# Delta rule of a hybrid decoder step: the sample group's state products moved to the first two turns, its new states accumulated in two parts

## The reference

```python
def step(S, inp):
    r_t, w_t, k_t, v_t, kk_t, b_t = inp
    sa = jnp.einsum('bhvk,bhk->bhv', S, kk_t)
    S = S * w_t[:, :, None, :] - sa[..., None] * b_t[:, :, None, :] + v_t[..., None] * k_t[:, :, None, :]
    return S, jnp.einsum('bhvk,bhk->bhv', S, r_t)
```

## Time and profile before

| what | value |
|---|---|
| median of 3 runs | 1483.42 us (1481.92 to 1490.57) |
| profiled execution | 1485.49 us |
| its span, first to last instruction | 1483.7 us |
| mean granted TensorE clock | 0.986 |
| TensorE busy (matmuls) | 1415.4 us, 95% |
| VectorE, ScalarE, GpSimd busy | 798.1, 578.4, 242.3 us |
| delta rule, first matmul to the next stage's first | 490.71 to 879.19 us |

### The profile page before, as it was taken

The page is one execution under the profiler, slowest core; times in us unless marked ns, Lnnn a source line. Parts: engine busy times, 40 slices in busy tenths (PEclk is TensorE's granted clock), DMA queues, the critical chain, the costliest instruction groups (busy, mean ns, idle before and its releaser), DMA issues. The chain is left out here.

```text
span 1483.7 us, 37543 instructions
## 1 busy us (share of the span) xinstructions
PE 1415.4 (95%) x16154; PEld 1284.7 (87%) x16154; DVE 798.1 (54%) x1592; ACT 578.4 (39%) x1182; POOL 242.3 (16%) x343
## 2 busy tenths in 40 slices
PE   7999999999999799999999989999999999998997
PEld 6989898887899799999999848899999997665885
DVE  6737245777821377777777564561111222775545
ACT  6626246887821122221222332441111132886324
POOL 0000000000000355654566230000001000214000
PEclk9999999999999999999999899999999998999999
DMA  5724122567692245434553146024334236431202
GB/s 205 223 59 103 59 89 89 161 174 225 193 261 87 59 110 117 107 86 108 117 117 89 53 149 229 29 78 145 91 98 116 67 119 168 150 103 33 87 29 93
DMA packets 244294, 173.47 MB, mean 117 GB/s; under 512 B 148735, under 2 KB 218303, under 8 KB 243215
## 3 DMA queue, kind: packets, MB, share of 16 engines
q1 hardware_dynamic: 212167, 156.12, 36.6%
q10 hardware_dynamic: 31968, 15.04, 3.5%
HBM read 110.97 MB, written 60.46 MB: 116 GB/s over the span
## 5 line engine op out<-in xcount | busy, mean ns | idle before, releaser
L366 PE MATMUL mix_acc<-mix_high,mix_w_high 128*128 128x364 f32 (+1 forms) x768 | 177.3, 339 | 11.5 <-ACT mix_high L432 10.3
L366 PE MATMUL mix_acc<-mix_low,mix_w_high 128*128 128x364 f32 (+1 forms) x768 | 171.5, 332 | 1.2 <-DVE mix_low L586 1.2
L366 PE MATMUL mix_acc<-mix_high,mix_w_low 128*128 128x364 f32 (+1 forms) x768 | 170.4, 330 | 0.0
L366 PEld LDWEIGHTS mix_acc<-mix_high,mix_w_high 128*128 128x128 f32 x768 | 129.6, 188 | 30.4 <-issue 28.6
L366 PEld LDWEIGHTS mix_acc<-mix_low,mix_w_high 128*128 128x128 f32 x768 | 132.5, 189 | 2.3 <-DVE mix_low L586 2.1
L366 PEld LDWEIGHTS mix_acc<-mix_high,mix_w_low 128*128 128x128 f32 x768 | 133.1, 188 | 0.2 <-DVE mix_w_low L600 0.2
L1482 PE MATMUL out_acc<-qkvg_room_r_high,qkvg_room_w_high 128*128 128x364 f32 (+1 forms) x320 | 105.8, 331 | 2.1 <-DVE qkvg_room_w_low L1834 2.1
L600 DVE TENSOR_TENSOR mix_w_low<-mix_wt,mix_w_high 128x1024 fp32r<-128x1024 f32 x32 | 39.2, 1224 | 124.9 <-ACT mix_w_high L438 124.6
L1482 PE MATMUL out_acc<-qkvg_room_r_low,qkvg_room_w_high 128*128 128x364 f32 (+1 forms) x320 | 105.1, 329 | 0.0
L1482 PE MATMUL out_acc<-qkvg_room_r_high,qkvg_room_w_low 128*128 128x364 f32 (+1 forms) x320 | 105.1, 329 | 0.0
L1832 DVE CAST qkvg_room_w_high<-qkvg_room_wt 128x1024 fp32r<-128x1024 f32 x20 | 14.0, 700 | 155.4 <-DMA qkvg_room_wt<-in_w_att 155.4
(11 more groups left out here) (278 smaller groups left out, 3418.3 us busy)
## 6 DMA issues: line engine op xcount, KB each, us to landing
mix_wt<-in_w_in SPq DMA_DIRECT2D x32, 512.0 KB, 4.6
qkvg_room_wt<-in_w_att SPq DMA_DIRECT2D x20, 512.0 KB, 3.7
delta_bk<-scr_bk SPq DMA_DIRECT2D x17, 512.0 KB, 4.7
delta_kr<-scr_kr SPq DMA_DIRECT2D x17, 512.0 KB, 7.1
scr_kr<-mix_outs SPq DMA_DIRECT2D x16, 512.0 KB, 3.8
scr_bk<-mix_outs SPq DMA_DIRECT2D x16, 512.0 KB, 4.5
early_xpad<-in_xpad SPq DMA_DIRECT2D x8, 548.5 KB, 8.8
scr_xg<-early_xs SPq DMA_DIRECT2D x8, 544.0 KB, 3.0
```

The costliest lines, as they stand in the source:

```text
L366: mm = pe.matmul(acc[:, s, k, 0:width], w[:, s, d, :], r[:, d, n0:n0 + width], start=d == 0 and q == 0, stop=d == DT - 1 and q == 2)
```

## The change

1. The eight loads of `s_sample` leave turns 1 to 8. SyncE issues them in the projections' last jobs, two each at n = 27 to 30 (`follow_slowly`). A copy of chunk 16's kr (`kr_own`, 512 KB) is loaded behind the first operands, at n = 26. `rows`, `s_sample` and `kr_own` move to the memory laid out by `first_of_delta`; `kr_own` shares its place with half of the inverse's buffer.
2. `turn_states` is cut into three: pairs 0 and 1 at the end of turn -1, pairs 2 to 4 and 5 to 7 in turn 0. They write into two banks that are free then, and ScalarE copies each out in turn 0 (`keep_own`). z of chunk 0 waits for the second copy, since it uses the bank.
3. `make_own_states` is cut into the products of v (`own_values`, which open the accumulation) and of u (`own_updates`, which close it). Pairs 0 to 3 of the first stand before and behind z of chunk 16 and behind its u; then come the turning of y 15, y 16, and the products of u.
4. `v_own` is made by GpSimd, in turn 15. All of `u_own` is made by ScalarE.
5. GpSimd scales `s_sample` by one pair at the end of each of turns 1 to 8, instead of all in turn 16.
6. VectorE adds the new states of pairs 0 and 1 before the norm of y 16, 2 and 3 inside it, and the rest behind it with the halves of the next weights. y 15 is turned and gated after z and u of chunk 16, not before.

```diff
+                    if G_ * DT + 2 < n < G_ * DT + 7:
+                        for pair in range(2):
+                            follow_slowly(sp, 2 * (n - (G_ * DT + 3)) + pair)
...
+        sp.dma_start(d["kr_own"][:], scr["kr"][TILES, :, :, :, 0:NB * NT]).then_inc(d["kr_own_loaded"], 16)
+
+    def load_states(sp, pair):
+        sp.dma_start(d["s_sample"][:, pair], a["s_sample"][:, pair]).then_inc(d["s_loaded"], 16)
...
-                    if 1 <= i <= DT:
-                        sp.dma_start(s_sample[:, i - 1], a["s_sample"][:, i - 1]).then_inc(s_loaded, 16)
...
+                    if front == SAMPLE:
+                        pool.wait_ge(v_loaded[SAMPLE % 3], 16 * (SAMPLE // 3 + 1))
+                        for b in range(NB):
+                            own = seq_mask[:, b:b + 1].rearrange("p (j n) -> p j n", j=1).broadcast_to([128, DT, 64])
+                            pool.tensor_tensor(v_own[:, b], v_rows[:, SAMPLE % 3], own, ALU.mult).then_inc(v_owned, 1)
+                    if 1 <= i <= DT:
+                        pair = i - 1
+                        pool.wait_ge(own_made, 2)
+                        end = keep["ends_sample"][:, pair, :].rearrange("p (b o) -> p b o", o=1).broadcast_to([128, NB, 64])
+                        pool.tensor_tensor(s_sample[:, pair], s_sample[:, pair], end, ALU.mult).then_inc(own_ended, 1)
...
                 def make_z(c):
                     if c == 0:
                         pe.wait_ge(zeroed, 3)
-                    elif c < SAMPLE:
-                        pe.wait_ge(s_kept, c)
+                        pe.wait_ge(own_kept, 2)
                     else:
                         pe.wait_ge(s_kept, c)
-                        pe.wait_ge(own_kept, 2)
...
+                def own_values(pairs):
+
+                    if pairs[0] == 0:
+                        pe.wait_ge(solved_wide, SAMPLE + 1)
+                        pe.wait_ge(rows_kept, 2 * SAMPLE + 2)
+                        pe.wait_ge(v_owned, NB)
+                    for pair in pairs:
                         if pair >= 4:
                             pe.wait_ge(own_done, pair - 3)
...
+                        for p in HALVES:
+                            pe.matmul((lm_bank + grown_bank)[pair % 4][p, :], rows[p, SAMPLE % 2, 1, pair, :], v_own[p, :, pair, :], start=True, stop=False)
+
+                def own_updates(pairs):
+                    if pairs[0] == 0:
+                        pe.wait_ge(u_owned, NB)
+                    for pair in pairs:
+                        for p in HALVES:
+                            mm = pe.matmul((lm_bank + grown_bank)[pair % 4][p, :], rows[p, SAMPLE % 2, 0, pair, :], u_own[p, :, pair, :], start=False, stop=True)
                         mm.then_inc(own_s, 1)
...
                     if behind == SAMPLE:
-                        for b in range(NB // 2):
+                        for b in range(NB):
                             act.wait_ge(u_kept, SAMPLE + 1)
                             act.activation(u_own[:, b], u[:], ACT.Copy, scale=seq_mask[:, b:b + 1]).then_inc(u_owned, 1)
...
+                        add_own((0, 1))
                         sum_squares(behind)
                         invert_root(behind)
+                        add_own((2, 3))
                         scale_y(behind)
...
+                        for pair in range(4, DT):
+                            add_own((pair,))
+                            if pair == DT - 1:
                                 gate_y(SAMPLE)
+                            for d in range(2 * pair - DT, 2 * pair - DT + 2):
+                                ahead["rest_of_weights"](dve, d)
```

More of the change, by code:

```diff
@@ L87, with mixed_projections @@
 HALF_K = N // 4
-def mixed_projections(nc, group, a, scr, keep, outp, g_stored, follow):
+def mixed_projections(nc, group, a, scr, keep, outp, g_stored, follow, follow_slowly):
     with Tensors(nc, "mix", group) as m:
@@ L772, in first_of_delta @@
         d["room"] = 8 * DT * 64 + 4 * DT * 64 + 3 * DT * 64 + sum(math.prod(shape) for shape in shapes.values()) + 64
+        d["rows"], d["s_sample"] = m.sb("rows", 128, 2, 2, DT, 64), m.sb("s_sample", 128, DT, NB, 64)
+        d["room"] += 4 * DT * 64 + DT * NB * 64
+        m.sb("inverse", 128, 2 * DT * 64)
+        d["kr_own"] = m.sb("kr_own", 128, 2, DT, 64)
+        d["s_loaded"], d["kr_own_loaded"] = m.sem("s_loaded"), m.sem("kr_own_loaded")
         d["consts_loaded"] = m.sem("consts_loaded")
@@ L799, in delta_rule @@
         kr, bk, v_rows = first["kr"], first["bk"], first["v_rows"]
-        rows, s_sample = m.sb("rows", 128, 2, 2, DT, 64), m.sb("s_sample", 128, DT, NB, 64)
+        rows, s_sample, kr_own = first["rows"], first["s_sample"], first["kr_own"]
         inv = m.sb("inv", 128, 2, 2 * DT * 64)
@@ L831, in delta_rule @@
         zeroed, gate_loaded = m.sem("zeroed"), [m.sem(f"gate_loaded{k}") for k in range(2)]
-        y_stored, s_loaded = [m.sem(f"y_stored{k}") for k in range(2)], m.sem("s_loaded")
+        y_stored, s_loaded, kr_own_loaded = [m.sem(f"y_stored{k}") for k in range(2)], first["s_loaded"], first["kr_own_loaded"]
         state_stored = m.sem("state_stored")
@@ L1002, in _ @@
                         scale_gain(behind)
-                    if i == SAMPLE:
-                        pool.wait_ge(own_made, 2)
-                        for pair in range(DT):
-                            end = keep["ends_sample"][:, pair, :].rearrange("p (b o) -> p b o", o=1).broadcast_to([128, NB, 64])
-                            pool.tensor_tensor(s_sample[:, pair], s_sample[:, pair], end, ALU.mult).then_inc(own_ended, 1)
                     if live(front):
@@ L1205, in _ @@
                         make_u(behind)
+                    if behind == SAMPLE:
+                        own_values((2, 3))
+                        turn_y(SAMPLE - 1)
                     if live(front):
@@ L1434, in _ @@
                     if behind == SAMPLE:
-                        dve.wait_ge(u_kept, SAMPLE + 1)
-                        for b in range(NB // 2, NB):
-                            own = seq_mask[:, b:b + 1].rearrange("p (j n) -> p j n", j=1).broadcast_to([128, DT, 64])
-                            dve.tensor_tensor(u_own[:, b], u[:], own, ALU.mult).then_inc(u_owned, 1)
+                        gate_y(SAMPLE - 1)
                     if live(front):
```

89 lines of the change are left out of this document (44 added, 45 removed).

## The result

The changed kernel takes 1472.97 us, median of 6 runs (1470.39 to 1479.06), against 1484.05 for the kernel before (1481.92 to 1490.57, 6 runs): ratio 0.9919, 95% interval 0.9897 to 0.9941, 11.1 us less where 10.1 were forecast. The profiled execution took 1473.34 us, its span 1471.6 against 1483.7.

The account below looks back on a forecast made before the run. TensorE was taken to bound the delta rule in its prompt turns, with time to be had at the two ends. Tail -12.1, start +2.0, GpSimd products 0, moved DMAs 0: -10.1 us, median 1473.3 us, range 1467 to 1480.

Parts of the forecast that it names:

- The products leave the end: Sample group's turn at the stage's end: without the 11.8 us of state products, z starts at 837.8 instead of 848.6.
- GpSimd's block: End of the stage: eight masked copies of v on GpSimd, 8 x 1.06 us, delay the last state's scaling and so z.
- L960's price rather than L1007's: GpSimd's eight products: 1.06 us each, not 1.26, which would make the end 1.6 us later.
- The end: Sample group's tail: VectorE's 13.0 us of work before the gate is later than TensorE; -12.1 us, at worst -10.5.
- the eight stay at 1.06: GpSimd's eight products: no contention with VectorE, whose solve and state sum each have PSUM in them.
- The start: Turns -1 and 0: state products partly fill TensorE's 2.15 and 3.91 us waits; cost +2.0 us, ends 0.7 and 5.4.
- no gap of over 1 us: Sign in the changed profile: TensorE has no gap of over 1 us between 496 and 506.
- that of the page +0.7: Start, by the skill page's clock rule: filling both gaps keeps 2.4 GHz, so the start costs 0.7 us.
- the emptier turns 1 to 8 gain something ... no row prices it: Turns 1 to 8, which lose eight state loads: a gain can't be excluded but was not priced, so 0.
- my rival: Turns 1 to 8: each gives back 0.5 us, -4 in all; with start at 0.7, total -15.4, 1468.0 us; chance 0.10.
- Job 29: Projections: the added kr load ahead of this job's weights costs 0 us, other end 2.4; slack 3.3 us.
- The slower rival: Turns -1 and 0: small products lower TensorE's clock for a turn or more; one turn makes 1488 us, two 1503; chance 0.04.

Follow-up runs that it names:

- Experiment 3: Changed kernel with four more GpSimd products, results unused, ahead of the eight masked copies of v; 1480.18 us, ratio 0.9993.
- experiment 6: Changed kernel with the eight v_own products of turn 16 back on ScalarE; 1472.74 us, ratio 0.9920.
- experiment 1: Kernel before the change with only the products of states made early, loads and scaling moved; 1475.36 us, ratio 0.9945.
- Experiment 7: Changed kernel with y and gate of turn 16 one pair earlier, at pair 6; 1472.84 us, ratio 0.9931.
- before: The kernel without the change, in its profiled execution; median 1484.05 us, profiled 1485.49 us.
- after: The changed kernel, unedited, in its first profiled execution; median 1472.97 us, ratio 0.9919, profiled 1473.34 us.
- experiment 4: Changed kernel with eight 256 KB loads of the sample states put back into turns 1 to 8, unread; 1473.43 us, ratio 0.9927.
- experiment 9: Changed kernel once more, unedited; 1472.46 us, ratio 0.9928.
- experiment 10: Changed kernel with eight unread loads of the sample states put back into turns 1 to 8, once more; 1475.49 us, ratio 0.9937.
- experiment 2: Kernel before the change with only the split new states and the moved copies of u and v, products of states left in turn 16; 1482.77 us, ratio 0.9999.
- experiment 5: Changed kernel with the 96 records of state products of pairs 5 to 7 issued three times; 1482.17 us, ratio 0.9994.
- experiment 8: Changed kernel with v_own on ScalarE, y and gate at pair 6, and pair 5 in the start's second gap; 1469.54 us, ratio 0.9911.
- experiment 11: Changed kernel with v_own on ScalarE, y and gate at pair 6, pair 5 in the second gap, once more; 1470.45 us, ratio 0.9913.
- experiment 12: Changed kernel with only pair 5 of the states' products moved from the start's third gap into the second; 1470.59 us, ratio 0.9914.
- the three edits: Changed kernel with v_own on ScalarE, y and gate at pair 6, and pair 5 in the second gap; two executions, 1469.54 and 1470.45 us.

## Why the prediction was right, and where it was not

**The products leave the end: right, with their cause.** The link that set z was GpSimd's block: forecast 8 x 1.06 = 8.48, measured 8.47 us. That it fits to the hundredth is luck: undisturbed the products came 1.00 us apart, and the last took 0.45 us more beside VectorE. Taking L960's price rather than L1007's decided 1.6 us. Shifted by the 0.7 us by which turn 16 starts later, the forecast times are 838.5 for z, 844.1 for u kept and 849.2 for the new states; measured 838.57, 843.86 and 848.96. Experiment 3 shows that the block is on the path, experiment 6 that only 0.65 us lie between it and the next limit (0.9 by the prediction). A part of this gain has a cause that the prediction left out: turning y 15 behind the products for u saved a wait of 4.16 us that would otherwise have opened (experiment 1). Its sum had the turning in the right place and so came out, but didn't say that it mattered.

**The end: -12.7 for -12.1.** VectorE does bound it: from the centring of y to the gate it took 12.77 us with no wait over 0.4, forecast 13.1, and it started 0.3 earlier. Experiment 7, which moves the gate ahead of 2.4 us of VectorE's own work, gains 1.9.

**A product I overlooked.** I took VectorE to read PSUM in all it does beside GpSimd's block. L1407 reads two operands from SBUF and took 1.54 us beside the block, 0.69 without. It ended at 835.8, before the scaling of the state, but it lengthened the last product of GpSimd's block from 1.04 to 1.49 us, and the block is on the path. So it cost up to 0.45 us, and the prediction's "the eight stay at 1.06" is wrong for one of them. The Trainium skill, page "SBUF — State Buffer", section "Who interferes with whom", says that a VectorE instruction with two SBUF inputs contends with a GpSimd instruction that reads SBUF. The trace agrees: here both got longer, VectorE's by 0.85 us. The copies of u show the same: 2.50 us for four in experiment 1 with GpSimd idle, 5.04 in before beside L1007.

**The start: +1.9 for +2.0, with a looser footing.** Added were 2.93 us (forecast 3.2), returned about 1 where I took the middle of 0 and 2.5. That it hit the tenth is partly luck: eight profiles of the same program up to there (after and experiments 1, 3, 4, 6, 7, 9, 10) gave 30.25 to 30.64 us six times and 32.1 twice, and the two of the old start (before, experiment 2) 28.39 and 29.02. In experiments 6 and 10 the clock was low twice, for 3.4 and then 6.8 us. The forecast "no gap of over 1 us" failed narrowly, with one of 1.16.

**Which rule for the clock.** Neither the page nor the rows tell it all. The Trainium skill, page "TensorE: Matmul & The Clock Gate", section "HAM oscillation — how this bites in real kernels", warns of idle gaps. Experiments 1 and 3 agree so far: the clock fell about 2 us into waits of 4.16 and 3.18 us. But in experiments 4, 5, 6 and 10 it falls between 515.3 and 516.6 us with no gap for 8 us or more, and with the start's gap filled it stayed up once (experiment 8) and fell twice (11 and 12). For the start, my reading of the rows gave +2.0 and that of the page +0.7; measured was +1.9.

**The term that failed: "the emptier turns 1 to 8 gain something ... no row prices it".** I set it to 0; it is -3.2 us on average over the profiles, of which 2.1 are in TensorE's waits, against -4 in my rival. There was a view that could have raised the question: TensorE's waits for "issue" in these turns, 5.6 us in all in before. So the forecast of the median was helped: by its own terms, as measured, it should have been -12.7 + 1.9 - 3.2 = -14.0, and the medians lie 11.1 apart, 11.9 beside experiment 9. What takes back 2 to 3 us isn't shown. One candidate lies outside the change: in 8 of the 12 profiles of changed kernels, and in neither of the two with the old program, the clock was low for 3.4 us at about 351 us, behind a wait for a load, and the delta rule began at 492.3 to 493.6 us instead of 491.1 to 491.6.

**Job 29: right, nearly used up.** Its weights were taken by ScalarE 3.4 us later, as this row of after shows beside the 446.58 of the earlier trace rows, and TensorE had no wait; the forecast slack was 3.3. In experiment 1 they were taken at 451.39, and that job took 12.3 us instead of 12.0.

```profile
449.99 1.06 ACT L441 ACTIVATE mix_w_high<-mix_wt 128x1024 fp32r<-128x1024 f32 x1 [7.94 <-DMA mix_wt<-in_w_in]
```

The slower rival didn't come: from 512 us to the end of the stage at 864, after runs at 1.00. In experiments 6 and 10 a short form of it did, 6.8 us at 0.50 right behind the small products.

## What to carry to other kernels

Follow an end as a chain, link by link over all engines, and price each new link by the row that is most like it; that gave this end to 0.6 us. Two halves of a change to the same chain don't add: one was worth 8.5 us, the other nothing alone and 4.2 behind the first, because taking work away laid bare a wait that the work had covered. And read an engine's waits that nothing releases: here they were 2 us shorter with the transfers moved out of these turns, though no instruction waited for a transfer. Look at more than one profile for such waits; two of the same kernel had 1.7 and 4.5 us.

## What the runs showed of the chip that I had not expected

A run of small products (64x16, 26 to 31 ns each) can lower TensorE's clock with TensorE fully busy: 77 records in 2 us, then 42. And the same program up to the same point can see the clock fall at 501.6 to 503.0 us, at 506.4 to 507.9, or only at 516.3 (experiment 4); of the two executions with the three edits one fell at 501.4 and one not at all, and their starts lie 4.5 us apart. In all executions of a changed kernel in which it fell early (experiments 3, 5, 6, 10, 11) the stage began at 492.3 us or later; but experiments 4 and 8 began at 492.85 and 492.38 and had no early fall. What chooses stays open.

An instruction of VectorE with both operands in SBUF and a GpSimd product that reads SBUF slow each other: 0.69 to 1.54 us for the one, 1.04 to 1.49 for the other.
